# A two-layer encoder on one core: first two up pieces of the feed-forward by token tile, and weight rings of 5 and 4

## The reference, cut to what matters

```python
    for l in range(DEPTH):
        h = rms_norm(x, attn_pre_norm[l])
        proj = jnp.einsum('bsd,dc->bsc', h, w_in[l])
        ...
        x = x + rms_norm(merged @ w_out[l], attn_post_norm[l])
        h = rms_norm(x, ffn_pre_norm[l])
        x = x + rms_norm(conv_gated_mlp(h, w_up[l], ffn_conv[l], w_down[l]), ffn_post_norm[l])

def conv_gated_mlp(h, w_up, conv_w, w_down):
    S = h.shape[1]
    u = h @ w_up
    pad = CONV_WIDTH // 2
    up = jnp.pad(u, ((0, 0), (pad, pad), (0, 0)))
    u = sum(up[:, t:t + S] * conv_w[t] for t in range(CONV_WIDTH))
    gate, val = jnp.split(u, 2, axis=-1)
    return (jax.nn.gelu(gate, approximate=True) * val) @ w_down
```

## Time and profile before

| what | value |
|---|---|
| median of three runs | 1046.75 us (1046.65 to 1047.1) |
| profiled execution, own time | 1046.71 us |
| its span, first to last instruction | 1044.8 us |
| mean granted TensorE clock | 0.999 of full speed |
| PE, DVE, ACT, POOL busy | 98%, 63%, 56%, 12% of the span |
| transfers | 163 GB/s in the mean |

### The profile page before, as it was taken

One profiled execution on the slowest core, in us unless ns is written; L12 is line 12 of the kernel. 1 busy time (PEld: TensorE's weight loads), 2 busy tenths in 40 slices (PEclk: granted clock), 3 DMA queues, 4 the chain that ended last, 5 costly groups with the idle time before them and its releaser, 6 DMA issues.

```text
span 1044.8 us, 15963 instructions
## 1 busy us (share of the span) xinstructions
PE 1025.7 (98%) x6332; PEld 918.9 (88%) x6332; DVE 656.4 (63%) x866; ACT 586.6 (56%) x843; POOL 121.7 (12%) x233
## 2 busy tenths in 40 slices
PE   8999999999999999999999999999999999999997
PEld 7889999888877999999898899998888789999996
DVE  5636556654585776776665355656556767676775
ACT  5666666556446645454475666565553466545453
POOL 3353114000000000000024321230000000000000
PEclk9999999999999999999999999999999999999999
DMA  8555445444453554546355544464445435554541
GB/s 253 178 180 158 128 128 190 142 143 161 142 190 112 202 201 162 203 160 220 103 191 163 165 129 124 149 201 161 138 148 178 163 139 179 185 201 163 201 161 41
DMA packets 106221, 170.79 MB, mean 163 GB/s; under 512 B 3377, under 2 KB 72804, under 8 KB 106148
## 3 DMA queue, kind: packets, MB, share of 16 engines
q1 hardware_dynamic: 104860, 166.88, 48.5%
q10 hardware_dynamic: 1208, 2.63, 0.7%
q0 software_dynamic: 80, 0.26, 0.1%
HBM read 168.72 MB, written 1.05 MB: 162 GB/s over the span
## 4 chain that ended last, share of the span: by engine, by line
PE 90%; DVE 4%; ACT 2%; DVEq 2%; issue 1%; POOL 0%; POOLq 0%; ACTq 0%
PE bank L1276 26%; PE bank L1278 26%; PE bank L1277 26%; PE bank L1566 2%; PE bank L1473 1%; PE bank L1494 1%; DVEq L1133 1%; PE bank L1559 1%; DVE merged L1134 1%; DVE hT_lo L1003 1%; PE bank L1482 1%; PE bank L1510 1%; PE bank L1255 1%; PE bank L1517 1%; PE bank L1556 1%
## 5 line engine op out<-in xcount | busy, mean ns | idle before, releaser
L982 DVE TENSOR_TENSOR w_lo<-w_raw,w_hi 128x2048 fp32r<-128x2048 f32 (+3 forms) x174 | 362.9, 2098 | 186.1 <-ACT w_hi L650 186.0
L650 ACT ACTIVATE w_hi<-w_raw 128x2048 fp32r<-128x2048 f32 (+3 forms) x174 | 302.4, 1752 | 49.8 <-PE bank L1278 49.2
L1276 PE MATMUL bank<-w_hi,hT_lo 128*128 128x512 f32 (+2 forms) x700 | 258.3, 369 | 0.7 <-DVE w_lo L982 0.6
L1278 PE MATMUL bank<-w_hi,hT_hi 128*128 128x512 f32 (+2 forms) x700 | 252.9, 361 | 0.0
L1277 PE MATMUL bank<-w_lo,hT_hi 128*128 128x512 f32 (+2 forms) x700 | 252.5, 361 | 0.0
L1276 PE MATMUL bank<-hT_hi,w_lo 128*128 128x256 f32 x704 | 199.9, 284 | 3.4 <-DVE hT_lo L1003 3.2
L1278 PE MATMUL bank<-hT_hi,w_hi 128*128 128x256 f32 x704 | 199.2, 283 | 0.0
L1277 PE MATMUL bank<-hT_lo,w_hi 128*128 128x256 f32 x704 | 199.2, 283 | 0.0
L1276 PEld LDWEIGHTS bank<-w_hi,hT_lo 128*128 128x128 f32 x700 | 131.5, 188 | 16.7 <-issue 2.0
L1278 PEld LDWEIGHTS bank<-w_hi,hT_hi 128*128 128x128 f32 x700 | 131.4, 188 | 14.1
L1277 PEld LDWEIGHTS bank<-w_lo,hT_hi 128*128 128x128 f32 x700 | 131.7, 188 | 13.0
(11 more groups left out here) (203 smaller groups left out, 1239.7 us busy)
## 6 DMA issues: line engine op xcount, KB each, us to landing
w_raw<-in_w_up_dram SPq DMA_DIRECT2D x44, 1024.0 KB, 4.9
w_raw<-in_w_in_dram SPq DMA_DIRECT2D x36, 1024.0 KB, 5.0
w_raw<-in_w_in_dram SPq DMA_DIRECT2D x36, 768.0 KB, 4.3
w_raw<-in_w_down_dram SPq DMA_DIRECT2D x22, 1024.0 KB, 5.3
w_raw<-in_w_out_dram SPq DMA_DIRECT2D x8, 1024.0 KB, 4.9
w_raw<-in_w_in_dram SPq DMA_DIRECT2D x8, 672.0 KB, 4.2
w_raw<-in_w_branch_mla_dram SPq DMA_DIRECT2D x4, 1024.0 KB, 4.9
w_raw<-in_w_branch_diff_dram SPq DMA_DIRECT2D x4, 1024.0 KB, 5.0
```

The costliest lines, as they stand in the source:

```text
L650: nc.scalar.activation(w_hi[:, n % RING, 0:nk * cols], raw[:, n % RING, 0:nk * cols], ACT.Copy).then_inc(hi_done, 1)
L982: V.tensor_tensor(w_lo[:, n % RING, s], raw[:, n % RING, s], w_hi[:, n % RING, s].bitcast(F32), ALU.subtract).then_inc(lo_done, 1)
L1276: PE.matmul(dst, lhs[1], rhs_hi, start=start, stop=False)
L1278: return PE.matmul(dst, lhs[0], rhs_hi, start=False, stop=stop)
```

## The change

The kernel does four things otherwise.

1. The first two up pieces are computed for tile 0 and then for tile 1 (`first_ups`), inside the step `mid`. Their matmuls stream the 128 tokens of one tile, in runs of two, out of `hT_hi` and `hT_lo`, and write the matching columns of banks 4 and 5. For tile 0 both pieces' first halves come in two parts of four channel blocks, then both second halves; then tile 1 is turned; then tile 1 follows. The step `turn` `ffn` and its dummy transposes are gone.
2. The copies from the turned banks are made for each tile (`ffn_hi`, `ffn_lo`), 16 instructions of 128 tokens on each engine instead of 8 of 256. Tile 0 is turned into banks 0, 1, 6 and 7, tile 1 into banks 2, 3, 0 and 1.
3. The scaling of x into `x_normed` moves from ScalarE to VectorE.
4. The low part is written over the raw weights, `w_low` lying on the bytes of `w_raw`. Raw and low now have five slots, high four; a transfer waits until PE has used the piece five back, a high part until it has used the piece four back. The split of the second up piece stands at its regular place, ahead of `mid`.

```diff
-WAITS = {"attn": (4, 14, 22), "ffn": (12, 24, 6)}
+WAITS = {"attn": (4, 14, 22)}
-RING = 3
+HI_RING = 4
+LOW_RING = 5
...
-    s += [("mid",), ("turn", "ffn")]
+    s.append(("mid",))
...
-        raw = sb("w_raw", [P, RING, 2048])
-        w_hi = sb("w_hi", [P, RING, 2048], F32R)
-        w_lo = sb("w_lo", [P, RING, 2048], F32R)
+        with ExitStack() as under:
+            raw = sb("w_raw", [P, LOW_RING, 2048], scope=under)
+        w_low = sb("w_low", [P, LOW_RING, 2048], F32R)
+        w_hi = sb("w_hi", [P, HI_RING, 2048], F32R)
...
+        def turned_bank(t, k):
+            return bank[((0, 1, 6, 7), (2, 3, 0, 1))[t][k // 2]][:, (k % 2) * P:(k % 2 + 1) * P]
+        def tile_tokens(cols, t):
+            return cols.rearrange("p (j r) -> p j r", r=4)[:, :, 2 * t:2 * t + 2]
...
-                    if l or n >= RING:
-                        sp.wait_ge(lo_done, l * NPIECE + (n + 1))
+                    if l or n >= LOW_RING:
+                        sp.wait_ge(piece_used, l * NPIECE + (HI_RING + n + 1 - LOW_RING))
...
+            def ffn_hi(l, t, pairs):
+                for pair in pairs:
+                    m = TURN_BEFORE["ffn"] + 4 * t + pair
+                    act.wait_ge(turn_full, l * NTURN + (m + 1))
+                    for k in (2 * pair, 2 * pair + 1):
+                        last = nc.scalar.activation(tile_tokens(hT_hi[:, k, :], t), turned_bank(t, k).rearrange("p (h j) -> p j h", h=2), ACT.Copy,
+                                                    scale=par_all[:, l, PRE_F + k:PRE_F + k + 1])
+                    last.then_inc(turn_hi, 1)
...
-                        pre_scale(l, 0)
+                        ffn_hi(l, 0, range(4))
                         pre_square(l, 1)
...
-                        pre_scale(l, 1)
+                        ffn_hi(l, 1, range(4))
...
                             post_gained(l, 0, t, 1)
+                            if t == 1:
+                                ffn_lo(l, 0, (0, 1))
                             post_add(l, 0, t)
-                            dve.wait_ge(ffn_squares, l * NT + (t + 1))
-                            mean(("pre", t), 2 * t)
+                            if t == 1:
+                                ffn_lo(l, 0, (2, 3))
+                            pre_scale(l, t)
+                        ffn_lo(l, 1, range(4))
...
+            def up_tile(l, c, j, t, ks):
+                n = UP0 + c
+                hi, lo = cut(w_hi, l, n), cut(w_low, l, n)
+                pe.wait_ge(lo_done, l * NPIECE + (n + 1))
+                for k in ks:
+                    if k % 2 == 0:
+                        pe.wait_ge(turn_emptied, l * NTURN + (TURN_BEFORE["ffn"] + 4 * t + k // 2 + 1))
+                    dst = tile_tokens(bank[4 + c][:, j * SEQ:(j + 1) * SEQ], t)
+                    a_hi, a_lo = tile_tokens(hT_hi[:, k, :], t), tile_tokens(hT_lo[:, k, :], t)
+                    w_of = slice(j * P, (j + 1) * P)
+                    PE.matmul(dst, lo[:, k, w_of], a_hi, start=k == 0, stop=False, skip_group_check=True)
+                    PE.matmul(dst, hi[:, k, w_of], a_lo, start=False, stop=False, skip_group_check=True)
+                    last = PE.matmul(dst, hi[:, k, w_of], a_hi, start=False, stop=k == 7, skip_group_check=True)
+                return last
+            def first_ups(l):
+                turn_ffn(l, 0)
+                for ks in (range(0, 4), range(4, 8)):
+                    for c in range(2):
+                        up_tile(l, c, 0, 0, ks)
+                for c in range(2):
+                    up_tile(l, c, 1, 0, range(8))
+                turn_ffn(l, 1)
+                for c in range(2):
+                    for j in range(2):
+                        last = up_tile(l, c, j, 1, range(8))
+                    last.then_inc(piece_used, 1)
```

More of the change, by code:

```diff
@@ L239, in emptied, with emptied_by_dve @@
     return who, sum(1 for m in DONE_ORDER[:DONE_ORDER.index(n) + 1] if (TILES[m][0] in BY_DVE) == (who == "dve"))
+def emptied_by_dve(m):
+    return sum(1 for x in DONE_ORDER[:DONE_ORDER.index(m) + 1] if TILES[x][0] in BY_DVE)
 N_DVE = sum(1 for x in TILES if x[0] in BY_DVE)
@@ L386, in build_trunk @@
         other_class = rope_b[:, 0:P]
-        raw_landed = [sem(f"raw_landed{i}") for i in range(RING)]
+        raw_landed = [sem(f"raw_landed{i}") for i in range(LOW_RING)]
         hi_done, lo_done, piece_used = sem("hi_done"), sem("lo_done"), sem("piece_used")
@@ L510, in _ @@
                     sp.sem_inc(slot_claimed, 1)
-                    sp.dma_start(cut(raw, n), weight_source(l, *piece)).then_inc(raw_landed[n % RING], 16)
+                    sp.dma_start(cut(raw, l, n), weight_source(l, *piece)).then_inc(raw_landed[(l * NPIECE + n) % LOW_RING], 16)
             store_rows(sp, 0)
@@ L1005, in empty_turn, with ffn_lo @@
-                    last.then_inc(turn_emptied, 1)
+                            last = V.scalar_tensor_tensor(out=lo[:, k0 + k, :], in0=src[:, k * SEQ:(k + 1) * SEQ],
+                                                          scalar=par_all[:, l, g0 + k0 + k:g0 + k0 + k + 1],
+                                                          in1=hi[:, k0 + k, :].bitcast(F32), op0=ALU.mult, op1=ALU.subtract)
+                    last.then_inc(turn_emptied, 1)
+            def ffn_lo(l, t, pairs):
+                for pair in pairs:
+                    m = TURN_BEFORE["ffn"] + 4 * t + pair
+                    dve.wait_ge(turn_hi, l * NTURN + (m + 1))
+                    for k in (2 * pair, 2 * pair + 1):
+                        last = V.scalar_tensor_tensor(out=tile_tokens(hT_lo[:, k, :], t), in0=turned_bank(t, k).rearrange("p (h j) -> p j h", h=2),
+                                                      scalar=par_all[:, l, PRE_F + k:PRE_F + k + 1],
+                                                      in1=tile_tokens(hT_hi[:, k, :], t).bitcast(F32), op0=ALU.mult, op1=ALU.subtract)
+                    last.then_inc(turn_emptied, 1)
@@ L1007, in negmax_of, with pre_scale @@
+            def pre_scale(l, t):
+                dve.wait_ge(ffn_squares, l * NT + (t + 1))
+                mean(("pre", t), 2 * t)
+                dve.wait_ge(roots_ready, l * 6 + (ROOT["pre", t] + 1))
+                for h in range(2):
+                    s = slice(h * 512, h * 512 + 512)
+                    V.tensor_scalar(xn[:, t, s], x[:, t, s], roots[:, ROOT["pre", t]:ROOT["pre", t] + 1], None, ALU.mult).then_inc(xn_done, 1)
             def negmax_of(l, p):
@@ L1208, in _ @@
                         kind, c, k0, nk, cols = PIECES[n]
-                        if n + 2 < NPIECE and n not in (OUT0 - 1, UP0 - 1):
+                        if n + 2 < NPIECE and n != OUT0 - 1:
                             split_lo(l, n + 2)
@@ L1299, in wait_turned @@
             def wait_turned(l, kind, c, k):
[L1301 removed]
+                what = {"mla": "attn", "uq": "latent", "ukv": "latent", "out": "merged"}.get(kind)
                 if what is None or c != 0:
@@ L1307, in use_first @@
             def use_first(n):
-                hi, lo = cut(w_hi, n), cut(w_lo, n)
+                hi, lo = cut(w_hi, 0, n), cut(w_low, 0, n)
                 k0, cols = PIECES[n][2], PIECES[n][4]
@@ L1384, in use_piece @@
                     for part in parts:
-                        hi, lo = cut(w_hi, part), cut(w_lo, part)
+                        hi, lo = cut(w_hi, l, part), cut(w_low, l, part)
                         p_k0, p_nk = PIECES[part][2:4]
@@ L1440, in turn, with turn_ffn @@
                     keep_clock(WAITS[what][NT], bank[3][:, 0:P])
+            def turn_ffn(l, t):
+                pe.wait_ge(tile_emptied_dve, BASE + l * N_DVE + emptied_by_dve(post_tile(0, 1, t)))
+                for k in range(KD):
+                    if k % 4 == 0:
+                        pe.wait_ge(xn_done, l * 4 + (2 * t + k // 4 + 1))
+                    last = PE.transpose(turned_bank(t, k), xn[:, t, k * P:(k + 1) * P], ident[:])
+                    if k % 2 == 1:
+                        last.then_inc(turn_full, 1)
+            def up_tile(l, c, j, t, ks):
+                n = UP0 + c
+                hi, lo = cut(w_hi, l, n), cut(w_low, l, n)
+                pe.wait_ge(lo_done, l * NPIECE + (n + 1))
+                for k in ks:
[20 more added lines that the diff above has]
+                    last.then_inc(piece_used, 1)
             def wait_t(l, key):
@@ L1541, in _ @@
                         turn_parameters()
+                    elif what == "mid":
+                        first_ups(l)
                     elif what == "w":
```

73 lines of the change are left out of this document (24 added, 49 removed).

## The result

The changed kernel took 1084.42 us in the median of four runs: 1066.37, 1075.63, 1093.21 and 1093.86, beside 1046.82 for the kernel before (median of four). It is slower by a different amount each time: the two lower runs alone give a ratio of 1.023 (95% interval 1.0179 to 1.0281), and the mean granted clock falls from run to run as the time grows, 0.989 in the run of 1066, 0.980 in that of 1076, 0.959 in those of 1093. Experiment 1 shows that this scatter belongs to the kernel.

The account below looks back on a forecast made before the run. PE, busy in 98% of the span, was taken as the bound, not the weight path. Per layer, matmuls +9.9 and waiting -4.3 gave +5.7; twice that, +11.4 on the time before, gave 1058.1 us, 8-in-10 range 1045 to 1074.

Parts of the forecast that it names:

- Narrow matmuls: First two up pieces: 192 matmuls of 128 tokens at 0.112 us replace 96 taking 11.6 us, +9.9 us per layer.
- loads-hidden rival: Weight loads pipeline under other matmuls, a narrow matmul costs 0.060 us: -1.9 per layer, 1042.8 us; chance 0.10.
- four-passes rival: A rounded matmul of 128 columns costs 0.225 us like an unrounded one: +26.7 per layer, 1100.1 us; chance 0.12.
- Waiting: PE's waiting and turning between output projection and third up piece falls from 10.1 to 5.8 us, -4.3 per layer.
- forecast +5.7: Stage from output projection to third up piece, per layer: matmuls +9.9 and waiting -4.3, ending at 867.6 against 861.94.
- waits between pairs: During tile 0's up matmuls, PE waits 0.4 us in all for later pairs of low copies.
- gap behind tile 1's turn: PE idles 1.15 us after turning tile 1, until its first low pair is copied.
- Tile 1's norm is hidden: Tile 1's normed rows are ready near 849.0, behind tile 0's matmuls lasting until 854.55, with 5 us to spare.
- The rings at nothing: Ring edits on the weight path cost nothing; PE's 0.6 us of waits is all a deeper ring can give back.
- The granted clock should stay at 1.00: Sign expected in the trace: PE's clock stays at 1.00 (2.4 GHz) despite only 0.9 us of turns before tile 0's matmuls.
- save nothing by themselves: The 42 dummies removed per layer lay inside the wait before the up matmuls, so removing them saves nothing.
- The rival: Clock lost: half of tile 0's 96 matmuls run at 1.2 GHz, +5.4 us per layer, 1068.9 us; chance 0.12.

Follow-up runs that it names:

- Experiment 1: The changed kernel with dummy transposes back in three waits per layer (7 and 8 around tile 0's turn, 8 behind tile 1's): 1057.36 us, ratio 1.0103.
- experiment 3: The kernel before, dummies kept, with each matmul of the first two up pieces split into two of 128 contiguous tokens: six runs, 1063.94 to 1103.35 us.
- experiment 2: The changed kernel with each narrow matmul streaming its 128 tokens twice, 256 columns with the same load: 1099.79 us, ratio 1.0507.
- experiment 5: The kernel before with the ring edits alone (five low slots over raw, four high ones): 1045.35 us, ratio 0.9987.
- experiment 9: The changed kernel with dummies only around the turn of tile 0 (7 ahead, 8 behind): 1056.99 us, ratio 1.0098.
- 10: The changed kernel with 8 dummies only behind the turn of tile 1: six runs, 1056.58 to 1066.81 us, ratio 1.0163.
- experiment 4: The kernel before without its 42 dummy transposes per layer ahead of the feed-forward: 1048.67 us, ratio 1.0018.
- Experiment 7: The changed kernel's rings, turns and copies by tile, but up matmuls 256 wide behind both tiles, with 7, 44 and 6 dummies: 1043.47 us, ratio 0.9972.

## Why the prediction was wrong

Forecast 1058.1 us, measured 1084.42. The direction held, and so did the sum at full clock; the clock did not.

- **Narrow matmuls, +9.9 per layer.** The mechanism was right, the size a little low: 11.2 + 11.5 us against 11.6 is +11.1. Measured 0.117 and 0.120 us in the changed kernel and 0.11 for tokens in a row (experiment 3), against 0.112. The loads-hidden rival (0.060) and the four-passes rival (0.225) are both out. What I had not seen is that the stream in runs of two costs as much as the load (experiment 2).
- **Waiting, -4.3 per layer.** Measured -5.5. That the stage as a whole came out at the forecast +5.7 (27.35 - 21.66) is in part luck, since the two errors cancelled. The copies cost 0.27 us, not 0.325 and 0.38, so the first narrow matmul came at 2.75 us instead of 3.1, there were no waits between pairs (0.4 forecast), and the gap behind tile 1's turn was 0.81 instead of 1.15. The matmuls were 6% dearer: 192 x 0.0065 = 1.2 us.
- **Tile 1's norm is hidden.** Right, with 6.6 us to spare.
- **The rings at nothing.** Off by 1.3 us (experiment 5). I looked only at waits for a weight; the gain was at waits for merged rows, through VectorE.
- **"The granted clock should stay at 1.00." This is the step that failed,** and with it the sentence that the removed dummies "save nothing by themselves": I asked what they save and not what they guard. Held at full clock, the changed kernel takes 1057.4 (experiment 1) or 1057.0 (experiment 9), within 1.1 of the forecast (the rings' unforeseen 1.3 us are in it). The missing 9 to 37 us are the clock. The rival was named, but with half of tile 0's matmuls at the lower level, +5.4 a time, and a chance of 0.12. One fall costs 9.2 us, because it lasts 20.5 us and runs on through tile 1's matmuls. For the higher runs no trace was taken; the steps between 1057, 1066, 1076 and 1093 are about one, two and four times 9, and their mean clock falls along with them (0.989, 0.980, 0.959). Counts of 1, 2 and 4 such stretches would fit, and so would fewer and longer ones, as the 40.9 us of experiment 3: that is argued from sums, not shown.

Why was it mis-sized? I read one row, the tail of the kernel before, where PE idles and the clock holds on for a while the earlier trace rows, and took the fall to be a matter of one long idle time, ended soon by work. Two things were missing. In these stages gaps of 0.7 to 1.2 us were enough when narrow matmuls followed, and the clock fell 1.7 to 2.8 us behind them, when unbroken work had already begun (changed kernel, experiments 3 and 10). And what follows decides the price: with 256-wide matmuls behind the gap the clock is back soon, at 2.1 us for the whole kernel (experiment 4), with narrow ones it is low for 20 to 41 us (changed kernel, experiments 3 and 10). In those three profiles it came back 4.6, 3.3 and 5.1 us behind the start of other work, wide matmuls or transposes. Whether narrow ones alone would ever let it return, no run shows. The change did both at once: it took the dummies out and put narrow matmuls behind the gaps. Neither alone was ruinous: the gaps cost 2.1 us, and narrow matmuls with the gaps filled cost only their own time.

And the change itself could not win in this form: a matmul that loads 128 columns costs the same with 128 tokens as with 256, so the work on tile 0 during the wait has to be paid again in full for tile 1. Experiment 7 is the direct measure.

## What to carry to other kernels

Splitting a matmul's streamed side below the point where its weight load is hidden buys no time: half the tokens cost 0.11 to 0.12 us where all of them cost 0.121, so work pulled forward in halves is work done twice. Before fillers are taken out of a wait, ask what stands behind it: here a low clock in front of 256-wide matmuls cost about 1 us per layer, in front of load-bound narrow ones 9 us and more, and not the same in every run, so read the clock of each run and not of the profiled one alone. The gain was in the other part of the idea: turns and copies by tile with wide matmuls behind both, and the critical tile's chain first (-5.1 us, 1.3 of it from the rings).
